# TensorE multiplies the next stage's first rounded weights by themselves between a norm's sums and its first product

## The chip, the cores and the metric

The kernel runs on one core of one Trainium2 chip. The metric is device time in microseconds (us); each figure is one execution of the whole program. The kernel before took 2057.76 us as the median of three runs, which lay between 2053.12 and 2065.13.

## The reference

A vector x of 256 tokens by 1024 features goes through two blocks of two layers each. Everything is float32.

- First block, per layer: three residual sub-layers, each opened by a norm. `f1` and `f2` are feed-forward parts (`silu(u @ wg) * (u @ wu)) @ wd`, width 2816); `m1` is a mixer of retention, stick-breaking attention and a state-space branch. Then a final norm, `fin`.
- Second block, per layer: `m2` (three attention branches with gates) and `f3` (feed-forward). Then the output norm, `out`.

Every norm is the same shape of work: for each token, the mean of the squares of its 1024 features, the inverse root of that mean, then for each feature `u = h * rs * gain * (1 + scale) + shift`. `scale` and `shift` come from a product of a condition vector with the large matrices `ada_w`, which the kernel makes on the side.

## The kernel before, in words

**Layout.** Features lie on the 128 partitions: h is eight tiles (d or k = 0 to 7) of 128 features by 256 tokens. A matrix product is eight products of 128x128 weights with a 128x256 tile, summed in a bank of PSUM.

**Precision.** A float32 weight is used as two rounded parts, `high` and `low`, and so is u (`m.uh`, `m.ul`, both in `u_split`). Each product of the reference is three on TensorE: high with high, high with low, low with high (`mm3`).

**Weights.** One stream of fills (SyncE's queue, into a ring of three slots) feeds grains of 128x1024 elements. For grain n ScalarE makes `high` (L1141), VectorE makes `low` by subtraction (L1576); four grains of each are held. A grain's `high` part may be written when TensorE has read grain n-4. The number behind a stage's name below is its layer: m1_0 is the first m1. Both engines work at most two or three grains ahead, in program order, among their other work.

**Stages.** `STAGES` is f1, m1, f2 (twice), fin, m2, f3 (twice), out: twelve norms. At the end of each, in order:

1. TensorE sums the squares with a tile of ones (`norm` in `pe_program`). After a feed-forward stage GpSimd has summed the first seven tiles, and two products are left; otherwise there are eight. Each is kept as two records of the profile. ScalarE writes the squares (L1158, or L1195 inside a feed-forward stage).
2. ScalarE makes the factor `rs` from the bank: a logarithm (L1162), an exponential (L1165).
3. For each k VectorE scales h (L1597), ScalarE adds the shift and rounds (L1179, `uh`), VectorE makes the rest (L1630, `ul`).
4. TensorE takes the first two grains of the stage together, k by k: six products (two grains, three products) as each k comes. These 48 products are called the first unit here. In a feed-forward stage the second unit starts with the third grain, whose `high` and `low` ScalarE and VectorE make after step 3. In an m1 stage a small unit of 24 products stands second, whose weights are 8 columns wide; its `low` part is 128x64 and takes a moment.

In the first stage the factor also waits, on ScalarE, behind the `high` of grains 0 and 1, which need the first fill; and VectorE is busy with sixteen pieces of `ada_w` (L1558).

**Order.** Each engine runs one list written out by hand; engines meet only at semaphores. Banks 0 to 3 are taken in turn for work; `("out", group)` says that a bank has been emptied.

**In m2 stages** GpSimd adds a window to a 128x2048 bias (L2084), whose DMA ScalarE issues when the stage before has ended.

Of the kernel before, what the change touches and what calls it, by code (L numbers as in the profile page):

```python
# [22 lines left out]
P = 128  # L23
D = 1024
KT = D // P
T = 256
# [40 lines left out]
GRAINS = 4  # L67
GRAIN = SLOT // 2
# [179 lines left out]
STREAM = Stream()  # L248
# [107 lines left out]
class Banks:  # L356
# [6 lines left out]
    def open(self, i, *group):  # L363
# [4 lines left out]
        self.pe.ledger.bank[group] = i  # L368
        return self.aps[i]

    def take(self, pool, *group):
        n = self.turn[pool]
        self.turn[pool] += 1
        return self.open(n % 4 if pool == "work" else 4 + n % 3, *group)
# [54 lines left out]
class Memory:  # L429
# [93 lines left out]
    def grain(self, n):  # L523
# [2 lines left out]
        s = n % GRAINS * GRAIN  # L526
        return [x[:, s:s + rows * cols].rearrange("p (k n) -> p k n", k=rows) for x in (self.high, self.low)]

    def grain_as(self, n):

        fill, view, rows, cols = STREAM.grains[n]
        src = view(self.slot_whole(fill))
        s = n % GRAINS * GRAIN
        hi, lo = self.high[:, s:s + rows * cols], self.low[:, s:s + rows * cols]
        hi, lo = (x.rearrange("p (k n) -> p k n", k=src.shape[1]) for x in (hi, lo))
        return src, hi, lo
# [63 lines left out]
STAGES = [(k, l) for l in range(LAYERS) for k in ("f1", "m1", "f2")] + [("fin", 0)] \  # L600
# [30 lines left out]
def after_ffn(s):  # L631

    n = STAGES.index(s)
    return n > 0 and STAGES[n - 1] in FFN


def square_slot(d):

    return 1 + (d - 1) % 3 if d else 0
# [6 lines left out]
def first_grain(s):  # L646

    kind, l = s
    if s in FFN:
        return "gate", FFN[s], 0  # L650
    return {"m1": ("xbc", l, 0), "m2": ("qa", l, 0), "fin": ("qa", 0, 0)}.get(kind)

def pe_program(pe, m):
    banks = Banks(pe, m.banks)

    def mm(out, lhs, rhs, start, stop):  # L660
        return pe.e.matmul(out, lhs, rhs, start=start, stop=stop, skip_group_check=True)  # L661
# [51 lines left out]
    def into_acc(s, keys, acts, ready, first, final):  # L713
# [14 lines left out]
        for k in range(2):  # L728
# [6 lines left out]
                        opens, False)  # L735
            t.then_inc(*pe.done(("read", n)))

    def norm(s):
        b = banks.take("work", "norm", s)
        if after_ffn(s):  # L740
            pe.wait_ge(("square_sum", s, KT - 2))
            mm(b[:, 0:T], m.ones[:, :], m.squares[:, 0, :], True, False)
            pe.wait_ge(("square", s, KT - 1))
            mm(b[:, 0:T], m.ones[:, :], m.squares[:, square_slot(KT - 1), :], False, True) \
                .then_inc(*pe.done(("square_read", s, KT - 1)))
            return
        for d in range(KT):
            pe.wait_ge(("square", s, d))
            mm(b[:, 0:T], m.ones[:, :], m.squares[:, d % 4, :], d == 0, d == KT - 1) \
                .then_inc(*pe.done(("square_read", s, d)))  # L750
# [298 lines left out]
    for d in range(0, KT, 2):  # L1049
        b = banks.open(4 + d // 2, "x", d // 2)  # L1050
# [5 lines left out]
    for s in STAGES:  # L1056
        norm(s)
        if s in FFN:
            ffn(s)
        elif s[0] == "m1":  # L1060
            mixer1(s)
        elif s[0] == "m2":
            mixer2(s)
    for a in range(TT):
        for g in range(2):
            b = banks.take("work", "y", a, g)
# [1085 lines left out]
def build(nc, dram):  # L2152
    ctx = ExitStack()
    m = Memory(nc, ctx)
    ledger = Ledger(m.sems)
    pe_program(Lane("pe", Dry(), ledger), m)
    act_program(Lane("act", Dry(), ledger), m, dram)
    dve_program(Lane("dve", Dry(), ledger), m)
# [5 lines left out]
    @block.tensor  # L2164
    def _(e):
        pe_program(Lane("pe", e, ledger), m)
# [188 lines left out]
```

## Time and profile before

| | |
|---|---|
| median of three runs | 2057.76 us |
| the profiled execution | 2061.55 us |
| its span, first to last instruction | 2059.7 us |
| TensorE busy | 1960.1 us, 95% |
| VectorE busy | 1437.0 us, 70% |
| ScalarE busy | 1017.1 us, 49% |
| mean granted TensorE clock | 0.978 |

The share of busy time says how full an engine is over the whole span. The granted clock is what part of TensorE's full rate of 2.4 GHz it was given: 1.00 is 2.4 GHz, 0.50 is 1.2 GHz. The views below are the chain of work that ended last, the waits, lists of instructions in order of time, and tables of stretches.

### The profile page before, as it was taken

The page shows a single profiled execution, that of the slowest core. Times are in us where ns is not written, and L with a number is a line of the kernel's source. Part 1 is how long each engine was busy: PE and PEld are TensorE (multiplying, and loading weights), DVE is VectorE, ACT ScalarE, POOL GpSimd, SP SyncE. Part 2 cuts the span into 40 slices and gives each one's busy share as a digit, 9 for nine tenths or more (in the row PEclk, how much of TensorE's full clock was granted, in tenths as well). Part 3 has the DMA queues.
Part 4 walks back from the last instruction along what each step waited for, and adds up shares of the span by engine and source line. Part 5 has one row for each costly group of instructions (what it writes and reads, how often), then busy time and mean ns, then how long its engine had stood idle before and what let it go on. Part 6 is the DMA issues. An engine that isn't in the chain of part 4 may idle for free.

```text
span 2059.7 us, 37419 instructions
## 1 busy us (share of the span) xinstructions
PE 1960.1 (95%) x15720; PEld 1907.2 (93%) x15720; DVE 1437.0 (70%) x2203; ACT 1017.1 (49%) x1565; POOL 116.2 (6%) x113
## 2 busy tenths in 40 slices
PE   4999999989999999999999979998999899999998
PEld 4999899989999999999899979998999899989998
DVE  6667787877677677878766757665777776656554
ACT  4444556454545544664544455453554454535443
POOL 0000002200000000022000010000000100000000
PEclk8999999999999999999999989999999999999999
DMA  8777565567786786755677745465678664554552
GB/s 333 288 255 284 209 235 194 186 222 263 253 308 218 256 294 228 257 185 195 225 256 253 280 165 205 161 220 204 217 269 283 229 222 158 207 208 159 184 189 98
DMA packets 83848, 466.35 MB, mean 226 GB/s; under 512 B 9440, under 2 KB 9568, under 8 KB 44512
## 3 DMA queue, kind: packets, MB, share of 16 engines
q1 hardware_dynamic: 47472, 330.78, 45.0%
q10 hardware_dynamic: 36208, 133.18, 18.3%
q8 instruction: 123, 2.02, 0.4%
q14 instruction: 45, 0.37, 0.0%
HBM read 462.88 MB, written 1.05 MB: 225 GB/s over the span
## 4 chain that ended last, share of the span: by engine, by line
PE 85%; DVE 8%; ACT 4%; DMA 1%; issue 1%; POOL 1%; ACTq 0%; DVEq 0%
PE bank L661 84%; DVE low L1576 3%; DVE ada_ring L1558 1%; DMA region<-ada 1%; ACT high L1141 1%; PE bank L930 1%; DVE u_split L1630 1%; DVE tmp L1597 1%; ACT u_split L1179 0%; POOL region L2075 0%; DVE region L2003 0%; DMA cond<-cond 0%; DVE region L1958 0%; ACT rs L1162 0%; DVE region L1719 0%
## 5 line engine op out<-in xcount | busy, mean ns | idle before, releaser
L661 PE MATMUL bank<-u_split,high 128*128 128x256 f32 x6464 | 1153.2, 283 | 45.0 <-DVE u_split L1630 39.0
L661 PEld LDWEIGHTS bank<-u_split,high 128*128 128x128 f32 x6464 | 998.0, 191 | 55.4 <-DVE u_split L1630 36.8
L1576 DVE TENSOR_TENSOR low<-ring,high 128x1024 fp32r<-128x1024 f32 (+1 forms) x600 | 732.2, 1229 | 376.4 <-issue 230.2
L661 PE MATMUL bank<-u_split,low 128*128 128x256 f32 x3232 | 908.4, 281 | 0.0
L1141 ACT ACTIVATE high<-ring 128x1024 fp32r<-128x1024 f32 (+1 forms) x600 | 602.6, 1046 | 102.5 <-PE bank L661 83.4
L661 PEld LDWEIGHTS bank<-u_split,low 128*128 128x128 f32 x3232 | 615.7, 191 | 0.5
L661 PE MATMUL bank<-hid,high 128*128 128x256 f32 x2112 | 364.5, 278 | 0.5 <-DVE low L1576 0.5
L661 PEld LDWEIGHTS bank<-hid,high 128*128 128x128 f32 x2112 | 319.9, 188 | 0.7 <-DVE low L1576 0.7
L1558 DVE SCALAR_TENSOR_TENSOR ada_ring<-ada_ring,cond 128x1024 f32<-128x1024 f32 x242 | 298.0, 1232 | 0.0
L661 PE MATMUL bank<-hid,low 128*128 128x256 f32 x1056 | 293.4, 278 | 0.0
L661 PEld LDWEIGHTS bank<-hid,low 128*128 128x128 f32 x1056 | 199.0, 188 | 0.0
L1207 ACT ACTIVATE sil<-bank 128x256 f32<-128x256 f32 x132 | 50.6, 384 | 264.9 <-PE bank L661 264.8
L1213 ACT ACTIVATE hid<-sil 128x256 fp32r<-128x256 f32 x132 | 55.3, 419 | 95.6 <-DVE sil L1679 95.6
L2045 POOL TENSOR_TENSOR tmp<-tmp 128x256 f32<-128x256 f32 x36 | 26.6, 738 | 1220.4 <-ACT tmp L1195 1220.4
L1195 ACT ACTIVATE tmp<-h 128x256 f32<-128x256 f32 x48 | 20.0, 418 | 138.5 <-DVE h L1667 138.5
L661 PE MATMUL bank<-region 128*128 128x256 f32 (+2 forms) x312 | 70.5, 352 | 4.7 <-DVE xa L1700 3.8
L661 PE MATMUL bank<-high,u_split 128*128 128x256 f32 (+1 forms) x384 | 69.0, 280 | 1.0 <-DVE low L1576 1.0
L661 PE MATMUL bank<-region,ring 128*128 128x256 f32 (+1 forms) x304 | 66.8, 380 | 0.0
L661 PEld LDWEIGHTS bank<-region 128*128 128x128 f32 (+1 forms) x312 | 53.8, 190 | 13.4 <-DVE xa L1700 4.6
L661 PEld LDWEIGHTS bank<-region,ring 128*128 128x128 f32 (+1 forms) x304 | 56.7, 187 | 9.1 <-ACT region L1490 0.5
L1597 DVE SCALAR_TENSOR_TENSOR tmp<-h,gcol,rs 128x256 f32<-128x256 f32 x88 | 40.8, 480 | 32.3 <-ACT rs L1165 32.2
L661 PEld LDWEIGHTS bank<-high,u_split 128*128 128x128 f32 x384 | 59.1, 188 | 1.2 <-ACT region L1352 1.2
(183 smaller groups left out, 1638.6 us busy)
## 6 DMA issues: line engine op xcount, KB each, us to landing
ring<-stream SPq DMA_DIRECT2D x302, 1024.0 KB, 5.8
ada_ring<-ada ACTq DMA_DIRECT2D x240, 512.0 KB, 4.3
region<-ada ACTq DMA_DIRECT2D x5, 1024.0 KB, 12.1
ring<-stream SPq DMA_DIRECT2D x4, 640.0 KB, 4.4
region<-ada SPq DMA_DIRECT2D x2, 1024.0 KB, 20.2
region<-na_bias ACTq DMA_DIRECT2D x2, 1024.0 KB, 5.9
ring<-stream SPq DMA_DIRECT2D x4, 512.0 KB, 4.7
cst<-const SPq DMA_DIRECT2D x1, 1600.0 KB, 11.6
```

The source lines that it names most:

```text
L661: return pe.e.matmul(out, lhs, rhs, start=start, stop=stop, skip_group_check=True)
L930: t = pe.e.transpose(b[:, k * T + a * P:k * T + (a + 1) * P], m.S[p][:, a * T + k * P:a * T + (k + 1) * P], m.c2("ident"))
L1141: act.e.activation(hi, src, ACT.Copy).then_inc(*act.done(("high", n)))
L1195: act.e.activation(m.squares[:, square_slot(d), :], m.hv[:, d, :], ACT.Square) \
L1207: act.e.activation(g, m.banks[act.bank("hid", f, n)][:, 0:T], ACT.Silu).then_inc(*act.done(("silu", f, n)))
L1213: act.e.activation(m.hid[0][:, n, :], g, ACT.Copy).then_inc(*act.done(("hid_high", f, n)))
L1558: dve.e.scalar_tensor_tensor(out=w, in0=w, scalar=1.0, in1=m.cond[:, block * D:(block + 1) * D], op0=ALU.mult, op1=ALU.mult, accum_out=m.s ...
L1576: dve.e.tensor_tensor(lo, src, hi.bitcast(F32), ALU.subtract).then_inc(*dve.done(("low", n)))
L1597: dve.e.scalar_tensor_tensor(out=out, in0=m.hv[:, d, :], scalar=gain[:, d:d + 1], in1=m.rs[:, 0:T], op0=ALU.mult, op1=ALU.mult).then_inc(* ...
L1630: dve.e.scalar_tensor_tensor(out=m.ul[:, e, :], in0=m.normed[:, e % 4, :], scalar=m.mod(shift)[:, e:e + 1], in1=m.uh[:, e, :].bitcast(F32) ...
L2045: pool.e.tensor_tensor(total, total, m.squares[:, square_slot(d), :], ALU.add) \
```

## The change

`idle` is new. After the sums of a norm TensorE waits for the `high` part of the next stage's first grain (not its `low`), and issues products of that part with itself: weights of 128 columns, taken in turn from its first four tiles, against the last 256-column half of its second 512 columns, into the work bank that the first unit opens next. It is the same form of product as those of the unit (128x128 by 128x256, rounded float32). Nothing reads the sums, and no semaphore is raised. There are 75 of them in the first stage and 18 in each other but `out`, which has no grain and gets none.

```
+    def next_work(self):
+
+        i = self.turn["work"] % 4
+        if self.group[i] is not None:
+            self.pe.wait_ge(("out",) + self.group[i])
+        return self.aps[i]
...
+    def grain_of(self, n):
+
+        return self.high[:, n % GRAINS * GRAIN:(n % GRAINS + 1) * GRAIN]
...
+IDLE, IDLE_FIRST = 18, 75
...
+    def idle(s):
+
+        key = first_grain(s)
+        if not key:
+            return
+        n = STREAM.index[key]
+        pe.wait_ge(("high", n))
+        w, b = m.grain_of(n), banks.next_work()
+        count = IDLE if STAGES.index(s) else IDLE_FIRST
+        for i in range(count):
+            mm(b[:, 0:T], w[:, i % 4 * P:(i % 4 + 1) * P], w[:, 2 * T:3 * T], i == 0, i == count - 1)
+
     def norm(s):
+        sums(s)
+        idle(s)
+
+    def sums(s):
         b = banks.take("work", "norm", s)
```

## Rows read from the trace of the kernel before

**Rows 1.** The page: engines' busy time, and the chain that ended last.
```profile
PE 1960.1 (95%) x15720; PEld 1907.2 (93%) x15720; DVE 1437.0 (70%) x2203; ACT 1017.1 (49%) x1565; POOL 116.2 (6%) x113
...
PE 85%; DVE 8%; ACT 4%; DMA 1%; issue 1%; POOL 1%; ACTq 0%; DVEq 0%
```
**Rows 2.** TensorE's waits over the span: us in total, times, longest.
```profile
PE bank L661 <- DVE u_split L1630: 39.0, 11, 13.2
PE bank L661 <- DVE low L1576: 21.4, 15, 4.0
```
**Rows 3.** In order of time, the gap at the first m1: start, us.
```profile
230.22 0.48 DVE L1630 SCALAR_TENSOR_TENSOR u_split<-tmp,mods,u_split 128x256 fp32r<-128x256 f32 x1 [0.18 <-ACT u_split L1179]
...
230.85 0.48 PE L661 MATMUL bank<-u_split,high 128*128 128x256 f32 x2 [2.69 <-DVE u_split L1630]
...
235.64 0.48 DVE L1630 SCALAR_TENSOR_TENSOR u_split<-tmp,mods,u_split 128x256 fp32r<-128x256 f32 x1 [0.18 <-ACT u_split L1179]
```
**Rows 4.** Table of stretches: length, engines busy, granted clock, DMA share, GB/s.
```profile
228.20:230.80 2.60, 0.00 (x0) 0.00 (x0) 1.46 (x4) 1.80 (x4) 0.00 (x0) 1.00 0.00 0
232.10:235.40 3.30, 3.30 (x18) 3.30 (x17) 3.30 (x9) 2.16 (x5) 0.00 (x0) 0.50 0.00 0
...
640.00:780.00 140.00, 140.00 (x1238) 140.00 (x1237) 101.16 (x143) 69.06 (x97) 2.22 (x3) 1.00 0.77 274
```
**Rows 5.** The same table, the first units of m1_0, f2_0, f1_1, m1_1, f2_1.
```profile
230.85:238.10 7.25, 7.25 (x48) 7.25 (x49) 6.53 (x17) 4.14 (x8) 0.00 (x0) 0.76 0.26 84
436.70:443.80 7.10, 7.06 (x48) 7.09 (x48) 6.38 (x15) 5.34 (x9) 0.00 (x0) 0.76 0.26 74
622.60:630.70 8.10, 8.05 (x49) 8.09 (x50) 7.39 (x15) 6.23 (x9) 0.00 (x0) 0.67 0.20 65
809.40:816.30 6.90, 6.90 (x48) 6.88 (x49) 6.72 (x18) 4.15 (x8) 0.00 (x0) 0.79 0.21 77
1010.20:1017.40 7.20, 7.20 (x48) 7.20 (x49) 6.49 (x15) 5.50 (x9) 0.00 (x0) 0.76 0.23 73
```
**Rows 6.** In order of time, f2_0's third grain on VectorE and the second unit's start.
```profile
442.55 2.36 DVE L1576 TENSOR_TENSOR low<-ring,high 128x1024 fp32r<-128x1024 f32 x2 [0.54 <-ACT high L1141]
...
443.87 0.46 PE L661 MATMUL bank<-u_split,high 128*128 128x256 f32 x2
```
**Rows 7.** In order of time, ScalarE in m1_0, later than its first unit.
```profile
246.60 0.60 ACT L1340 ACTIVATE region<-bank 128x512 f32<-128x512 f32 x1 [4.39 <-PE bank L661]
```
**Rows 8.** In order of time, m2_0's second unit, then m2_1: GpSimd's bias and VectorE.
```profile
1223.04 0.50 PE L661 MATMUL bank<-u_split,high 128*128 128x256 f32 x2 [0.37 <-DVE low L1576]
...
1632.25 5.94 POOL L2084 TENSOR_TENSOR region<-region,cst 128x2048 f32<-128x2048 f32 x1 [10.44 <-DMA region<-na_bias]
...
1633.90 4.58 DVE L1630 SCALAR_TENSOR_TENSOR u_split<-tmp,mods,u_split 128x256 fp32r<-128x256 f32 x1 [0.18 <-ACT u_split L1179]
```
**Rows 9.** The sums after fin, in order of time; then the table of that stretch.
```profile
1206.83 6.11 PE L661 MATMUL bank<-tmp,ones 128*128 128x256 f32 x16 [6.59 <-ACT tmp L1158]
...
1201.50:1211.60 10.10, 4.77 (x11) 3.82 (x12) 3.15 (x9) 7.58 (x17) 2.07 (x1) 0.50 0.30 105
```
**Rows 10.** First stage, in order of time: ScalarE's first grains, VectorE, TensorE.
```profile
29.50 2.00 ACT L1141 ACTIVATE high<-ring 128x1024 fp32r<-128x1024 f32 x2 [6.27 <-DMA ring<-stream]
...
38.28 0.55 PE L661 MATMUL bank<-u_split,high 128*128 128x256 f32 x1 [13.19 <-DVE u_split L1630]
43.07 0.48 DVE L1630 SCALAR_TENSOR_TENSOR u_split<-tmp,mods,u_split 128x256 fp32r<-128x256 f32 x1 [0.18 <-ACT u_split L1179]
44.09 2.36 DVE L1576 TENSOR_TENSOR low<-ring,high 128x1024 fp32r<-128x1024 f32 x2 [0.53 <-ACT high L1141]
46.73 0.40 PE L661 MATMUL bank<-u_split,high 128*128 128x256 f32 x2
```
**Rows 11.** Table of stretches of the first stage.
```profile
38.20:44.20 6.00, 5.92 (x28) 5.95 (x29) 5.29 (x14) 4.21 (x8) 0.00 (x0) 0.50 0.83 350
46.70:60.00 13.30, 13.30 (x115) 13.30 (x114) 8.69 (x13) 7.16 (x11) 0.00 (x0) 1.00 0.81 267
```

## The prediction, made before the changed kernel was run

> **What bounds the kernel now.** I read the page's busy times and chain first: TensorE is busy 95% of the span and has 85% of the chain [rows 1]. So the time changes only with TensorE's pace or its idle time. The waits come next. It waited 39.0 us in 11 places for VectorE's `u_split` [rows 2], of which ten are the gaps of this change. The one in m1_0 shows the pattern: 2.69 us in which nothing runs on TensorE, then the first unit [rows 3]. Nine stages have it; the first stage has the long gap of 13.2 us; 1.6 us is a late u tile in m2_1; together 39.0. (fin feeds no products, and out's are not weights.) The change leaves the gap as it is and fills it. A third view says what the filling can be for, the table of stretches with its granted clock. It is 1.00 (2.4 GHz) in m1_0's gap, with no product in it, and 0.50 (1.2 GHz) in 232.1 to 235.4, where TensorE is busy all the time; at the unit's end it is full again [rows 4]. Every first unit has its low stretch: the means over the units are 0.67 to 0.79 [rows 5].
>
> **What a product costs.** At the full clock 1238 products fill 140 us [rows 4], 113 ns each; a unit's own, at 115 in 13.3 us [rows 11], take 116. At the low clock it is 28 in 5.92 us [rows 11], 211 ns.
>
> **The gaps after the change.** 18 products take 18 x 0.116 = 2.1 us at the full clock. That ends 0.6 us before the 2.69 us are over, so no real product is late by it. Two waits are added. That for `high` is met: the grain's `low`, made from it, is ready before the gap. That for the bank is one which the unit's own `banks.take` makes anyway, with three groups of work between. Behind them on TensorE stands only the unit, which waits for u until the gap's end. Other engines wait for nothing that the filler does: no semaphore, no DMA. Added instructions: 9 x 18 + 18 (fin) + 75 = 255 products.
>
> If TensorE has work through the gap I expect that the clock stays full and the low stretch after it goes. The reason is from the same rows: the clock fell after the gap and never in the long busy stretches, such as the 140 us at 1.00 [rows 4].
>
> **What a first unit gains.** Its pace has three limits, and the clock is only one.
>
> - *u.* VectorE delivers u tiles from 230.22 to 235.64 [rows 3], seven steps of 0.77 us. The last is done at 236.12, and six products (0.70 us) follow. So even at the full clock the unit takes 236.12 + 0.05 + 0.70 - 230.85 = 6.0 us and not 48 x 0.116 = 5.6.
> - *The clock.* With its low stretch it takes 7.3 us in m1_0, 6.9 in m1_1, 7.1 in f2_0 and f3_0, 7.2 in f2_1 and f3_1, 8.1 in f1_1 ([rows 5]; the two f3 units have the values of the two f2 units).
> - *The next grain.* In a feed-forward stage the second unit needs the third grain. Its `low` starts on VectorE at 442.55 and, the first of two in 2.36 us, is ready 1.15 us later, at 443.70; the second unit started at 443.87 [rows 6]. The `high` and `low` stand in ScalarE's and VectorE's lists behind the u tiles, which don't depend on TensorE. So the second unit can't start before 443.75 or so, 7.0 us after the first product at 436.74, whatever the clock.
>
> | stage | unit before | can be | gain |
> |---|---|---|---|
> | m1_0 | 7.3 | 6.1 | 1.2 |
> | m1_1 | 6.9 | 6.1 | 0.8 |
> | f1_1 | 8.05 | 7.1 | 0.95 |
> | f2_0, f3_0 | 7.1 | 7.05 | 0.05 each |
> | f2_1, f3_1 | 7.25 | 7.1 | 0.15 each |
> | m2_0 | 7.4 | 7.4 | 0 |
> | m2_1 | 10.1 | 10.1 | 0 |
>
> In m2_0 the second unit already waits 0.37 us for `low` [rows 8], which VectorE makes after the u tiles. In m2_1 GpSimd's 5.94 us bias sum and one u tile of 4.58 us (it takes 0.48 elsewhere) lie over each other [rows 8]; the last u tile is so late that the clock doesn't matter. Sum: 1.2 + 0.8 + 0.95 + 0.1 + 0.3 = 3.35, taken as 3.4 us.
>
> Does it stay won? In the feed-forward stages TensorE does not wait afterwards. In m1_0 the next wait of some size comes at 253 us, for `low`; but ScalarE, which it hangs on, waited 4.39 us for TensorE at 246.60 [rows 7], so it comes earlier too. I keep all of m1's 2.0 us; the other end is none of it, were later waits in m1 (L1576, 21.4 us over the whole span [rows 2]) set by VectorE alone.
>
> *fin.* Its filler runs while VectorE and ScalarE write h, and nothing is late. The sums after it run at 0.50: 16 records in 6.11 us [rows 9]; the same 16 take 3.62 us elsewhere, so 2.5 us could be had if the clock stayed full until 1206.8. But the filler (2.1 us) ends near 1202.3 and leaves 4.5 us idle, more than the 2.69 us that brought the clock down in the other gaps. I take 0; the ends are 0 and 2.5.
>
> **The first stage.** The filler waits for `high` of grain 0, ready 1.0 us after 29.50 [rows 10], so it starts at 30.55. The clock is low then and rose in the unit after 5.9 us of products [rows 11]. So I bound its rise in the filler by m1_0's 3.3 us [rows 4] and this stage's own 5.9:
>
> - after 3.3: 16 products at 211 ns, 59 at 116: 10.2 us, end at 40.7;
> - after 5.9: 28 and 47: 11.4 us, end at 41.9.
>
> The first real product could go at 38.28 [rows 10]. It goes 2.4 to 3.6 us late. The 48 products then run at 116 ns without waiting for u (the last tile is done at 43.55 [rows 10], 30 products behind the start need nothing later): 5.6 us, end at 46.3 to 47.5, against 46.73 now. The grain for the second unit is there at 45.3. So it is -0.4 to +0.8; I take +0.7, near the end that comes from this stage's own stretch. 75 is too many here: the late start eats what the clock gives.
>
> **Sum.** -3.4 + 0.7 = -2.7 us. The profiled execution took 2061.55 us (span 2059.7), so 2058.9 under the profile. It lay 3.8 us above the median of the three runs; against that median it is 2055.1 us, 0.13% faster. About 0.5%, 10 us, is what a measurement of this kernel can tell from no change, so I expect "no change".
>
> The Trainium skill (TensorE: Matmul & The Clock Gate, Terms) puts the price of the low clock at the throttled time times one minus the clock's share, half of it here. From the means in rows 5 that rule gives 1.7 + 1.7 + 2.7 + 1.4 + 1.7 us for the five units shown, and about 17 us with the other four, where I count 3.4; the sum would be 2061.55 - 17 + 0.7, less 3.8, or 2041.5 (beside rival 1). The rule takes TensorE to be what its own work waits for; here u and the third grain are.
>
> **Rivals.**
>
> 1. *All of the low stretch comes back.* Then every unit takes 6.05 us: 1.2 + 0.8 + 2.0 + 2 x 1.05 + 2 x 1.2 + 1.35 (m2_0) = 9.85, less 0.7: -9.2, 2048.6 us. For it: TensorE has 85% of the chain. Against: f2_0's second unit starts 0.1 us behind its grain. Chance 0.08.
> 2. *m1's gain is lost later in the stage*, where TensorE waits for `low` and for `xa`: -1.4 + 0.7 = -0.7, 2057.1. Chance 0.16.
> 3. *The fall is only put off.* The filler leaves 0.6 us at its end, and the first unit is fed at 0.77 us for 0.70 of work. If that, or products whose sums nobody uses, don't hold the clock, the low stretch falls behind the first unit, where neither u nor a grain hides it: 16 products of a 3.3 us stretch lose 95 ns each, 1.5 us in each of nine stages, 13.7, with 0.7 of the first stage: +14.4, 2072. It is slower than before from two such stages on. Against: before the gap TensorE also had idle time of 0.6 us between two sums and the clock stayed at 1.00. Chance 0.06.
> 4. *The change doesn't do what it says:* the clock falls as before, in the same place. Then only the first stage counts, where a clock that stays low gives 75 x 0.211 = 15.8 us, end at 46.4, and 48 x 0.211 = 10.1: end at 56.5, +9.8 in all, 2067.5. Chance 0.02.
>
> The forecast itself has 0.68.
>
> **How the numbers follow.** The forecast's own range is 2055.1 with -3.6 / +2.1 for the ends above (fin and first stage; m1 and first stage) and some 5 us for a median of three, since the three runs before lie 12 us apart. With rivals 1 and 2 inside, the range is 2048.5 to 2062.5; rivals 3 and 4 are left out. Faster by over 0.5% (below 2047.5) needs rival 1 and some luck: 0.09. Slower by over 0.5% (above 2068) is rival 3, half of 4, and a share of the spread: 0.08. Within 0.5%: 0.83.
>
> **What would show it.** Right: granted clock near 1.00 in the first units of m1_0 and f2_0, the low stretches gone; gap to the first real product unchanged from the sums in nine stages; m1_0's unit near 6.1 us but f2_0's second unit starting 7.1 us after its first product, now with an idle time of about a microsecond released by `low` (L1576); the first stage's first real product 2.4 to 3.6 us late and its unit's end near 47. Wrong: units of 6.05 us in feed-forward stages (rival 1), a stretch at 0.50 inside the second or third unit (rival 3), or first real products later than before in the nine gaps.

## The result: 0.55% faster, where no change was forecast

The changed kernel took 2054.58 us (median of 12 runs, 2040.97 to 2058.91), the kernel before 2059.78 us on the same chips (12 runs, 2053.12 to 2071.35). The ratio is 0.9945, with a 95% interval of 0.9919 to 0.9972: 6 to 17 us, 11 by its middle (5.2 by the two medians). The forecast was 2055.1 us and -2.7 us. That 2054.6 lies so near 2055.1 is luck: twelve runs of the kernel before gave a median 2 us above that of the first three. Here and below a ratio leaves out executions in a slow state, which medians include; the one profile of e7 fell in such an execution (4017 us), so that its row has no counts.

The page of the profile after, whose span is 2047.2 us (the changed kernel's product line is L676):

```profile
PE 1970.1 (96%) x15975; PEld 1916.5 (94%) x15975; DVE 1437.6 (70%) x2203; ACT 1017.2 (50%) x1565; POOL 116.8 (6%) x113
```

255 products more, and TensorE's busy time is only 10 us above [rows 1]; the new ones alone need 255 x 0.117 = 30. So the others took less, at the low clock and otherwise. TensorE's waits, as us in total, times, longest:

```profile
PE bank L676 <- DVE low L1607: 24.8, 20, 4.0
...
PE bank L676 <- DVE u_split L1661: 9.4, 10, 3.7
...
PE bank L676 <- ACT high L1172: 4.4, 1, 4.4
```

The wait for u fell from 39.0 [rows 2] to 9.4 us, since the filler lies in it. That for `low` rose by five places: the second units. In order of time, the gap at m1_0, then the start of f2_0's second unit:

```profile
223.96 2.50 PE L676 MATMUL bank<-high 128*128 128x256 f32 x18
...
227.00 0.47 PE L676 MATMUL bank<-u_split,high 128*128 128x256 f32 x2 [0.54 <-DVE u_split L1661]
...
438.04 0.50 PE L676 MATMUL bank<-u_split,high 128*128 128x256 f32 x2 [0.75 <-DVE low L1607]
```

18 products end 0.54 us before the first real one (forecast: 0.6). The table of stretches for the first units of m1_0, f2_0, f1_1, m1_1, f2_1, against [rows 5]:

```profile
226.90:233.50 6.60, 6.50 (x51) 6.34 (x52) 5.89 (x16) 4.28 (x9) 0.00 (x0) 1.00 0.18 60
430.90:437.00 6.10, 6.04 (x47) 5.97 (x48) 5.38 (x14) 4.35 (x8) 0.00 (x0) 1.00 0.12 34
623.60:629.70 6.10, 6.07 (x48) 5.98 (x48) 5.38 (x14) 4.38 (x8) 0.00 (x0) 1.00 0.13 37
809.50:815.50 6.00, 5.97 (x47) 5.88 (x48) 5.82 (x16) 4.16 (x8) 0.00 (x0) 1.00 0.12 29
1009.30:1015.40 6.10, 6.02 (x48) 5.94 (x48) 5.38 (x14) 4.32 (x8) 0.00 (x0) 1.00 0.13 33
```

The clock is 1.00 in all five and a unit takes 6.0 us, as the second limit had it; but the feed-forward second units then wait.

**Where the 12 us between the two profiles are.** TensorE streams at one of two steady paces. In the lists of one line's products (min/median/max in ns) they show as two durations; here f2_1 before, f1_1 before, f2_1 after and f2_0 after:

```profile
L661 PE MATMUL bank<-u_split,high x642: 281/281/281, 1016.7 to 1129.9; 128*128 128x256 f32 x161
```
```profile
L661 PE MATMUL bank<-u_split,high x590: 276/276/276, 639.9 to 739.9; 128*128 128x256 f32 x197
```
```profile
L676 PE MATMUL bank<-u_split,high x666: 276/276/281, 1016.9 to 1129.9; 128*128 128x256 f32 x167
...
L676 PE MATMUL bank<-u_split,high x634: 281/281/281, 444.9 to 556.6; 128*128 128x256 f32 x159
```

A stage is at one or the other for a thousand products and more. The step from one product's start to the next is 113.4 ns where the duration is 276, and 117.8 ns where it is 281. ScalarE's `silu`, once in 48 products, shows it in the lists by time; f2_1 before, then after:

```profile
1051.56 0.38 ACT L1207 ACTIVATE sil<-bank 128x256 f32<-128x256 f32 x1 [2.23 <-PE bank L661]
1057.21 0.38 ACT L1207 ACTIVATE sil<-bank 128x256 f32<-128x256 f32 x1 [2.23 <-PE bank L661]
```
```profile
1054.87 0.39 ACT L1238 ACTIVATE sil<-bank 128x256 f32<-128x256 f32 x1 [2.01 <-PE bank L676]
1060.31 0.39 ACT L1238 ACTIVATE sil<-bank 128x256 f32<-128x256 f32 x1 [2.01 <-PE bank L676]
```

5.65 against 5.44 us a unit. From ScalarE's first u tile (L1179, after L1210) to that of the next stage, a feed-forward stage other than the first takes 185.9 us all at 113 and 192.7 all at 118, in both kernels, and 188.0 with only its down part at 118 (e17, e1). In the first profile before, f2_1 and f3_1 are at 118 and f1_0 is in its gate and up part; after, f2_0 alone.

By the start times of all products, 5879 of the kernel before run at 118 and 2825 of the changed one. At 4.4 ns each that is 25.9 and 12.4 us: a difference of 13.5 us, against 12.5 between the spans.

### The profile page after: what moved, and what is told of

Same layout as the page of the kernel before. It is cut to its first block, busy times and chain, and to the rows that moved or that the text cites. A ratio compares the mean times of both kernels' runs of the same rounds, so it can differ in the third digit from the quotient of the medians.

```text
span 2047.2 us, 37929 instructions
## 1 busy us (share of the span) xinstructions
PE 1970.1 (96%) x15975; PEld 1916.5 (94%) x15975; DVE 1437.6 (70%) x2203; ACT 1017.2 (50%) x1565; POOL 116.8 (6%) x113
## 3 DMA queue, kind: packets, MB, share of 16 engines
HBM read 462.88 MB, written 1.05 MB: 227 GB/s over the span
## 4 chain that ended last, share of the span: by engine, by line
PE 84%; DVE 9%; ACT 4%; DMA 1%; issue 1%; POOL 1%; SPq 0%; DVEq 0%; ACTq 0%
PE bank L676 83%; DVE low L1607 3%; DMA ring<-stream 1%; DVE u_split L1661 1%; ACT high L1172 1%; DVE tmp L1628 1%; DVE ada_ring L1589 1%; PE bank L961 1%; ACT u_split L1210 0%; POOL region L2106 0%; DVE region L2034 0%; DVE region L1989 0%; ACT rs L1193 0%; PE bank L1100 0%; ACT rs L1196 0%
## 5 line engine op out<-in xcount | busy, mean ns | idle before, releaser
L676 PE MATMUL bank<-u_split,high 128*128 128x256 f32 x6464 | 1132.4, 280 | 19.7 <-DVE low L1607 10.3
L676 PEld LDWEIGHTS bank<-u_split,high 128*128 128x128 f32 x6464 | 980.3, 188 | 30.0 <-DVE low L1607 11.1
L676 PE MATMUL bank<-u_split,low 128*128 128x256 f32 x3232 | 897.3, 278 | 0.0
L676 PEld LDWEIGHTS bank<-u_split,low 128*128 128x128 f32 x3232 | 606.7, 188 | 0.4
L676 PE MATMUL bank<-hid,high 128*128 128x256 f32 x2112 | 361.9, 277 | 0.7 <-DVE low L1607 0.7
L676 PEld LDWEIGHTS bank<-hid,high 128*128 128x128 f32 x2112 | 318.8, 188 | 0.9 <-DVE low L1607 0.9
L676 PE MATMUL bank<-hid,low 128*128 128x256 f32 x1056 | 292.4, 277 | 0.0
L676 PEld LDWEIGHTS bank<-hid,low 128*128 128x128 f32 x1056 | 198.2, 188 | 0.0
L676 PE MATMUL bank<-region 128*128 128x256 f32 (+2 forms) x312 | 70.5, 352 | 4.7 <-DVE xa L1731 3.8
L676 PE MATMUL bank<-high,u_split 128*128 128x256 f32 (+1 forms) x384 | 69.2, 280 | 1.5 <-ACT region L1276 1.5
L676 PE MATMUL bank<-region,ring 128*128 128x256 f32 (+1 forms) x304 | 66.8, 380 | 0.0
L676 PEld LDWEIGHTS bank<-region 128*128 128x128 f32 (+1 forms) x312 | 53.8, 190 | 13.4 <-DVE xa L1731 4.5
L676 PEld LDWEIGHTS bank<-region,ring 128*128 128x128 f32 (+1 forms) x304 | 56.7, 187 | 9.1 <-ACT region L1521 0.5
L676 PEld LDWEIGHTS bank<-high,u_split 128*128 128x128 f32 x384 | 59.1, 188 | 1.7 <-ACT region L1276 1.6
```

## Experiments

Two theories. **P, pace:** the pace is settled where the stream is broken and stays until the next break, and the change makes the break another one. **D, direct:** only the direct gains count, the rest is luck. "At 118" is the number of products in steady stretches at that pace in the run's one profile; "stages at 113" are feed-forward stages whose gate and up part runs at 113 from the second or third unit on. Medians and the median of the kernel before are in us; two rows with different values of it were timed on different chips or at different times. A break is given from product start to product start; the idle time in the lists is some 0.3 less.

| run | median | before | ratio (95%) | at 118 | stages at 113 |
|---|---|---|---|---|---|
| before, first profile | | | | 5879 | 3 of 6 |
| e12 before again | 2069.7, one run | 2059.8 | | 7716 | 2 |
| changed, first profile | 2054.6 | 2059.8 | 0.9945 (0.9919-0.9972) | 2825 | 5 |
| e13 changed again | 2050.5, one run | 2059.8 | | 3846 | 5 |
| e17 changed again | 2054.3 | 2063.2 | 0.9955 (0.9924-0.9987) | 4376 | 5 |
| e1 gaps only | 2044.4 | 2059.2 | 0.9941 (0.9917-0.9964) | 2680 | 6 |
| e16 gaps only | 2046.1 | 2063.2 | 0.9925 (0.9889-0.9962) | 1791 | 6 |
| e2 first stage only | 2062.1 | 2059.2 | 1.0016 (0.9990-1.0042) | 8386 | 2 |
| e6 six products | 2061.4 | 2062.8 | 0.9973 (0.9950-0.9997) | 5348 | 4 |
| e7 thirty products | 2053.5 | 2062.8 | 0.9954 (0.9929-0.9980) | | |
| e11 thirty, profile | 2056.3, one run | 2059.8 | | 4111 | 5 |
| e5 third grain early | 2055.8 | 2059.2 | 0.9984 (0.9955-1.0012) | 8361 | 2 |
| e14 the same and a wait | 2052.1 | 2063.2 | 0.9950 (0.9921-0.9979) | 3156 | 6 |
| e3 wait, no filler | 2053.8 | 2059.2 | 0.9981 (0.9961-1.0001) | 1975 | 6 |
| e10 wait for fourth grain | 2064.2 | 2059.8 | 1.0017 (0.9981-1.0052) | 4551 | 5 |
| e9 gaps and wait | 2048.9 | 2062.8 | 0.9927 (0.9896-0.9957) | 2940 | 6 |

The seven ratios of kernels that keep the clock up by 18 or 30 products and have the break ahead of the second unit are 0.9925 to 0.9955. The other five are 0.9973 to 1.0017. e4 and e15, one profile each, are in the text.

### Parts of the change: e1, e2, e16, e17

```
e1, e16:  IDLE, IDLE_FIRST = 18, 0
e2:       IDLE, IDLE_FIRST = 0, 75
```

> The 18 products in each later gap stay, the 75 ahead of the first stage go. Two theories. Theory P (pace): TensorE streams these products at one of two steady paces, 113 or 118 ns each; the pace is drawn where the stream is broken, stays until the next break, and a rise of the clock inside a running stream gives the 118 more often than a resumption at the full clock does. In the two profiles at hand 5879 products of the kernel before and 2825 of the changed one run at 118 ns, which is 13 us at 4.4 ns each. Theory D (direct): only the direct gains count, 3.4 us of first units in the later stages and -0.7 us of the first stage; the rest of the measured difference is the luck of the draw. P: the later stages (f2_0 to f3_1) show the 113 pace in at least 4 of 5 feed-forward stages, f1_0 keeps its clock rise inside the first unit; time 5 to 9 us below the kernel before. D: 3.4 us below.

> Only the 75 products ahead of the first stage stay; the later gaps are empty. P: the later stages are as in the kernel before, with 118 ns in about half of them; the first stage's gate and up part is at 113 ns more often (4.7 us when it is) and its unit ends 0.7 us later, so 1 to 4 us below the kernel before. D: 0.7 us above it.

The later gaps carry the gain; the 75 products carry none. Both sums were too small for e1 (14.9 us below by medians, 12 by the ratio). e2 came out 2.9 us above, with an interval of 2 below to 9 above, where P had 1 to 4 below and D 0.7 above: nearer to D, and its first stage was at 113. But e1's later stages are as P said, 5 of 5 at 113, and e2 has 1 of 5.

> e1_gaps_only again, on the same chip and beside the changed kernel, to tell the two apart. By the stage lengths of the profiles the 75 products take the first stage's pace to 113 ns in all four profiles that have them, and cost 0.7 us there; without them it was at 113 in four of six. So on the mean 0 to 1 us between the two, either way; the first comparison had e1 10 us below the changed kernel's median, which I expect not to hold.

> The changed kernel again, timed beside e16 on the same chip. P: 6 to 12 us below the kernel before; within 3 us of e16.

e17 gave the changed kernel's gain again. On one chip e16 was 8 us below it by medians, more than was expected; the intervals overlap (runs of 2043.0 to 2059.9 and 2042.6 to 2069.1), so that the 75 products cost more than their 0.9 us is likely and not shown.

### Number of products: e6, e7, e11

```
e6:       IDLE, IDLE_FIRST = 6, 0
e7, e11:  IDLE, IDLE_FIRST = 30, 0
```

> 6 products in each later gap instead of 18, none ahead of the first stage. They take 0.7 of the 2.7 us. P: the clock falls as in the kernel before, TensorE then has its clock rise inside the first unit, no long idle time ahead of the second unit, and 118 ns in about half of the stages: within 3 us of the kernel before. If filler of any length gave the gain, it would be some 10 us below.

Mostly as P said. The clock falls in all five later feed-forward stages, the break ahead of the second unit is under 0.2 us, and 3 of the 5 are at 113. The gain is 1.4 us by medians but 6 by the ratio (1 to 10), so that P's "within 3 us" is open.

> 30 products in each later gap, none ahead of the first stage: 30 x 0.117 = 3.5 us against a gap of 2.7, so the first real product is 0.8 us late in nine stages. Step of the prediction on test: in feed-forward stages the second unit starts when the third grain is ready, 7.05 us after the u tile's, whatever TensorE does; then its idle time ahead of it shrinks from 1.05 to some 0.5 us and the five stages lose nothing, while m1 loses 0.3 us each. Time equal to that of e1_gaps_only within 2 us as long as the shorter idle time still leaves the 113 ns pace; were TensorE's own work the bound, 0.8 x 9 = 7 us above it.

> 30 products in each later gap, none ahead of the first stage, for its profile. The first real product is some 0.8 us late in nine stages; if the third grain is the bound of a feed-forward stage's start, the second unit starts no later against the u tiles than with 18 products, and the idle time ahead of it is 0.3 to 0.7 us; were TensorE the bound it would start 0.8 us later.

The third grain is the bound. The start of f2_0's second unit in e11:

```profile
438.50 0.51 PE L676 MATMUL bank<-u_split,high 128*128 128x256 f32 x2 [0.73 <-DVE low L1607]
```

It stands 8.26 us behind ScalarE's first u tile (430.24); with 18 products 8.26 too (429.78, 438.04), in all five stages. The idle time did not even shrink (0.73 and 0.75), since the products that come late wait for the last u tiles anyway; I had expected 0.3 to 0.7. f2_0, f1_1 and f3_0 last 185.9 us, as with 18 products, so in these stages the 0.8 us of a late start costs nothing. The timed forecast of e7 missed all the same: not within 2 us of e1 but 9 us above it by medians, 3 by the ratios. The profiles put this down to pace (4111 products at 118 in e11, 2680 and 1791 in e1 and e16); less 4.4 ns for each the spans are 2036.4, 2036.3 and 2034.6 us.

### The break ahead of the second unit: e5, e14

```
e5, look_ahead in act_program and dve_program:
-            split(STREAM.index[key] + AHEAD)
+            split(STREAM.index[key] + AHEAD + (key[0] == "gate" and key[1] > 0))
e14: e5, and in ffn of pe_program, ahead of a unit:
+            if n == 1 and f:
+                pe.wait_ge(("silu", f, n - 1))
```

> The changed kernel, with the third grain of each feed-forward stage but the first rounded ahead of the norm's factor instead of behind the u tiles, so that the second unit need not wait for it (it waits about 1 us in five stages). P: the break after the first unit is gone, the pace which the u-fed first unit leaves (often 118) stays for the stage, and the time is equal to or above that of the changed kernel in spite of the 5 us saved. D: the second unit starts 1 us earlier in five stages, less some 0.3 us that the factor comes later: 3.5 us below the changed kernel, some 14 below the kernel before.

This tells the theories apart most sharply. The wait of 0.8 us in five stages is gone, four of those stages run at 118, and the median is 1.2 us above the changed kernel's instead of 3.5 below. D's 14 us below the kernel before lie outside the interval (9 below to 2 above). Without the pace e5 is the best of all: its span of 2064.5 less 8361 x 4.4 ns is 2027.7 us, 6 below the changed kernel's on the same reckoning.

> e5_third_grain_early with one wait more: in the five later feed-forward stages TensorE waits ahead of its second unit for ScalarE's silu of the first, which comes some 1.5 to 2 us after the unit's end. So the third grain is early, the idle time is back, and nothing else is added. P with the idle time of 0.9 us or more as what gives the 113 ns pace: four or five of the five stages start at 113 where e5 had one; 5 x 1.8 = 9 us of waits are paid and some 20 us of pace come back against e5's profile, so the median is 2 to 9 us below that of e5 (2055.8). D: 9 us above it.

TensorE's waits name the new wait, 5.6 us in all. In order of time, f1_1's; then that stage's durations in e14 and in e5:

```profile
627.96 0.39 PE L676 MATMUL bank<-u_split,high 128*128 128x256 f32 x1 [1.11 <-ACT sil L1240]
```
```profile
L676 PE MATMUL bank<-u_split,high x590: 276/276/277, 639.7 to 739.9; 128*128 128x256 f32 x197
```
```profile
L676 PE MATMUL bank<-u_split,high x568: 281/281/281, 639.8 to 739.9; 128*128 128x256 f32 x190
```

All five stages are at 113. 5.6 us of waits were added, and the median is 3.7 us lower (ratios 0.9950 and 0.9984). The two were timed on different chips and their intervals overlap; from them e14 stands between 15 us below e5 and 1 above, as an estimate. So that a wait makes this kernel faster is likely and not shown. That it does not cost its 5.6 us, let alone D's 9, is.

### Waits without filler: e3, e4, e10, e15

```
in ffn of pe_program, kernel before, ahead of a unit:
e3:   if n == 2:      pe.wait_ge(("silu", f, n - 1))
e4:   if n % 3 == 2:  pe.wait_ge(("silu", f, n - 1))
e10:  if n == 1:      pe.wait_ge(("low", STREAM.index["up", f, 1]))
e15:  if n % 3 == 2:  pe.wait_ge(("prod", f, n - 1))
```

> The kernel before, without filler; in each of the six feed-forward stages TensorE waits once, ahead of the third unit, for ScalarE's silu of the second unit (some 0.6 us idle at the full clock). P: the pace is drawn anew there and is 113 ns in most of the six stages, so the six waits (3.5 us) are paid back by about one or two stages at 4.7 to 7 us each: 1 to 7 us below the kernel before. D: 3.5 us above it, since waits only cost.

Six of six stages at 113, 5.5 us below the kernel before by medians, 4 by the ratio (the interval just reaches 1). D's 3.5 us above lie outside it. But the waits are not shown to have done it. In five of the six stages the second unit, ahead of the wait, was at 113 already, as in f2_1 here; only in f1_1 did the pace change at the wait, from 118 to 113.

```profile
L661 PE MATMUL bank<-u_split,high x28: 276/276/276, 1012.3 to 1016.8; 128*128 128x256 f32 x28
```

> The kernel before, without filler, where TensorE waits for ScalarE's silu of the unit before ahead of units 3, 6, 9, 12, 15, 18 and 21 of each feed-forward stage: 42 idle times of about 0.75 us at the full clock, seen in the profile. P, made narrower by the first four experiments: a stream that starts after an idle time of 0.7 us or more runs at 113 ns, so at least 38 of the 42 stretches behind a wait are at 113. If the draw is a coin's whatever the idle time, about 21 to 28 are. Time: 42 x 0.75 = 31 us for the waits, less up to 20 for the pace: 5 to 25 us above the kernel before.

The narrow form of P fell here. Behind 42 breaks of 0.75 us the pace was 113 about as often as 118 (of 43 long stretches behind such breaks 21 at 113). One profile, 2102.7 us. It was no coin either: inside the stages the pace changed at 35 of the 36 waits that followed another of these, from 113 to 118 and back in turn. In e3, e9 and the two profiles of the kernel before all 9 long stretches behind a break of 0.75 us were at 113, six of them with 113 ahead of it too. So a break can change the pace, and a break of 0.75 us left either; what chooses is not its length alone, and draws in one execution are not independent.

> The kernel before, no filler. In each feed-forward stage TensorE also waits for the low part of the fourth grain ahead of its second unit, which is ready some 1.1 us after the third; so it idles about 1 us there, as the changed kernel does, but with the clock falling in the first unit as before. P, as the profiles so far have it: behind an idle time of 0.9 us or more 22 of 23 long stretches ran at 113 ns, behind shorter breaks about half; so at least 5 of the 6 stages start at 113. Four waits of 1.1 us and two shorter ones cost 5 us, the pace gives about 11: 4 to 9 us below the kernel before. D: 5 us above it.

Five of six stages at 113 as P had it, and yet no gain: 4 us above the kernel before by medians, which is D's number and not P's (interval 4 below to 11 above). Less its products at 118 the span is 2047.3 us, 13 above the kernel before. 6.5 of that are six waits of 1.1 (27.9 us in 21 places for `low`, against 21.4 in 15 [rows 2]). The rest lies in part with the clock, as the table of stretches shows: in f1_1 (and at 1458 in f3_0) it falls not in the first unit but behind the wait, in the second, where nothing else hides it.

```profile
636.10:639.40 3.30, 3.30 (x18) 3.30 (x17) 3.24 (x6) 1.75 (x3) 0.00 (x0) 0.53 0.82 288
640.00:643.40 3.40, 3.40 (x33) 3.40 (x32) 0.00 (x0) 0.61 (x2) 0.00 (x0) 1.00 0.82 294
```

The same break is harmless in the changed kernel, whose filler has kept the clock up ahead of it.

> e4_many_stalls with the wait on VectorE's product instead of ScalarE's silu: 42 idle times of some 1.2 to 1.5 us instead of 0.75. In e4 the stretches behind them were at 113 and at 118 about equally. If a longer idle time itself makes the 113 ns pace (22 of 23 behind 0.9 us or more so far), at least 36 of the 42 are at 113. If the idle ahead of the second unit is special for another reason (the table load, the u tiles before it), about half are, as in e4.

It missed its purpose in the main: the breaks were 3.3 us, the clock fell behind most of them (mean 0.947, 2278 us), and the pace then came from the clock's rise, some 25 times 113 and 14 times 118. Behind six of them the clock stayed at 1.00. These are a test of length, and it went against it: five of the six stretches ran at 118 and one at 113. The products behind the first of them, which followed on 3.06 us of idle time and on a unit at 113:

```profile
L661 PE MATMUL bank<-u_split,high x89: 281/281/281, 55.4 to 70.9; 128*128 128x256 f32 x89
```

A longer break does not by itself make the pace of 113.

### Both, and the kernels again: e9, e12, e13

```
e9: e1, and in ffn of pe_program:
+            if n == 2 and f == 0:
+                pe.wait_ge(("silu", f, n - 1))
```

> e1_gaps_only with one wait more, in the first stage ahead of its third unit (the silu of the second), 0.75 us. P: the first stage, whose clock rises inside its first unit, is then at 113 ns always instead of about half the time: 4.7 us in half of the runs for 0.75 us, so 1.5 us below e1_gaps_only on the mean and less spread. D: 0.75 us above it.

All six stages at 113, but e1 had that too, and the first stage was at 113 ahead of the wait already. e9 is 4.5 us above e1 by medians and 3 below by the ratios: nothing to choose between them.

> The kernel before once more, to see how the pace falls in another execution. P: 118 ns in two to four of the six feed-forward stages, others than in the first profile, and 40 to 60% of all products that run at either pace at 118. D: the same stages as before, as a property of the code.

> The changed kernel once more. P: behind the idle time of 1 us ahead of the second unit at least four of the five later feed-forward stages start at 113 ns; under 30% of the products at 118. D: f2_0 at 118 again, as a property of the code.

The stages at 118 are others: in e12 f1_0, f2_1, f3_0 and f3_1, in e13 f2_1 and not f2_0. It is no property of the code. e12's 1837 more products at 118 are 8.1 us, its span is 8.2 longer.

## Why the prediction was wrong

**The failed step** is "What a product costs". It gave the full clock two prices, 113 ns from [rows 4] and 116 from [rows 11], and took them for one thing measured in two places. They are the two paces. (A table of stretches also counts the records that reach over its ends: 113 products start in the 13.3 us of [rows 11], which is the 118 ns pace, and 1235 in the 140 us of [rows 4], which is 113.4.) The sum then took the pace of all products outside the first units as unchanged, without a reason. More than a third of the kernel's products stood at the dearer one, 26 us of the span, and nothing in the sum could move them. That TensorE was 85% of the chain [rows 1] should have made its pace the first question.

**What moved them.** In the kernel before a later first unit ends with the clock's rise inside it and no break, or one under 0.3 us, ahead of the second. In the changed kernel the clock stays up, the first unit ends 1 us early, and TensorE waits for the third grain: a break of 1.05 us. The prediction saw this wait and priced it as a gain forgone. The gain goes with it. Later stages at 113: 36 of 40 in the eight profiles with filler (e14's wait included) and such a break; 9 of 20 without (before, e12, e2, e6); 1 of 5 in e5, with filler and without the break. (In e12 at f1_1 and in e2 at f2_1 the clock did not fall; these two had the break by themselves and are at 113.) The starts also show the pace on both sides of the break. Of the 40 stages the first unit's last products were at 118 in 13, and 12 of these went on at 113; 27 were at 113, and 3 of these went on at 118. Over all profiles but e4's and e15's, 52 of 59 long stretches (100 products or more) behind a break of 0.9 us or more at the full clock were at 113, and 6 of 18 behind one of 0.14 to 0.3. e15's six, above, don't fit.

**Does it add up?** Span less 4.4 ns for each product at 118: 2033.9 and 2034.0 us in the two profiles of the kernel before, 2034.8, 2031.8 and 2034.3 in the three of the changed one. The means differ by 0.3 us. The counts differ by 3115 on the mean, 13.7 us; the timed difference is 6 to 17 us. So in these five profiles the whole gain is pace. The term of -2.7 us is not contradicted and not confirmed by 0.3, with 3 us between profiles.

**Point by point.**

- *The gap, the clock:* right. Gaps keep their length, the low stretches of the first units are gone, but for m2_1's, which comes behind the late u tile (6.8 us at 1629.6).
- *u and the third grain as limits:* right. The unit takes 6.0 us; the second starts 7.1 us behind the first product (430.96, 438.04); feed-forward stages at 113 last 185.9 us in both kernels.
- *f1_1, m1:* f1_1 186.7 to 185.9 us (0.95 forecast), m1_1 200.8 to 199.8 (0.8), m1_0 205.9 to 204.0 (1.2); but e12, without filler, had 185.9 in f1_1, for its clock did not fall there. For m1 one pair of profiles shows little: in the six with 18 products and the third grain late m1_0 took 202.5 to 206.1 us.
- *fin, m2_0:* 12.7 and 12.8 us, 227.6 and 227.4: nothing, as forecast.
- *The first stage:* right in kind and size. In order of time:

```profile
30.61 11.45 PE L676 MATMUL bank<-high 128*128 128x256 f32 x75 [4.35 <-ACT high L1172]
41.90 0.40 PE L676 MATMUL bank<-u_split,high 128*128 128x256 f32 x2
```

  The first real product was 3.6 us late or a little less, and the stage took 188.7 us, against 187.8 in e1 and 187.9 in e16 at the same pace: +0.9, forecast +0.7.
- *Rivals:* 1 fell: the first units were shorter, but the feed-forward stages gained only what the third grain allows. 2 stays open, with m1's scatter. 3 did not come true here; e10 has the low stretch behind the first unit, by an added wait. 4 fell: the clock stayed up. The rule of the Trainium skill (TensorE: Matmul & The Clock Gate, Terms), half the throttled time, gave 2041.5 us. The traces do not agree: 2054.6 us was measured, and apart from the pace 0.3 us came back, since u and the third grain bind. With the third grain early (e5) it is 6 us.

**Still open.** What inside TensorE makes the two paces, and what chooses one at a break. Shown is that the pace can change at a break, and that the break of 1 to 1.4 us ahead of the second unit goes with 113 (36 of 40). That this is the break's length is not shown: 0.75 us left 113 nine times in nine elsewhere and alternated in e4, and 3.3 us left 118 five times in six in e15. What comes ahead of the break (a unit fed at u's pace, or full units) was not varied by itself. The counts of one execution are not independent draws, either. The best version measured is the gaps alone (e1, e16: 0.9941 and 0.9925 of before).

## What to carry to other kernels

If an engine is the bound, first ask whether its price per instruction is the same in every stage: two numbers for one form, 4% apart, are a lead and not scatter. A kernel whose runs lie 12 us apart may get such a price anew in each stage, and then one profile of it is one sample; compare stage by stage, and count. Look at the price ahead of an added wait too, before the wait is given the credit (e3). An edit that moves a wait of the bound engine can change more than the wait.

## What the runs showed of the hardware

- Products of 128x128 by 128x256 in rounded float32, each with its weight load, stream at 113.4 or 117.8 ns at the full clock, for up to 1568 in a row, through changes of unit, bank and operands. Recorded durations are 276 and 281 ns; one weight load in three is 192 instead of 188 ns at the slower pace.
- The pace changes where the stream is broken (break or clock rise) and at the passage from the gate and up part to the down part, where it sometimes changed without a break to speak of (steps of 115 and 124 ns, in f2_0 and f1_1 of e1).
- With 18 products whose sums nobody reads in a gap of 2.69 us the clock stayed at 1.00 through the gap and the first unit in eight of nine stages; in the ninth, m2_1, it fell 8 us behind the first real product in the first profile, after the late u tile. With 6 it fell in all five feed-forward first units and in m1_0's; with none, in nine of nine in the first profile before and in eight in e12.
